# Expert weights loaded as whole matrices into four places instead of quarters into sixteen

## The reference, cut to what matters

```
def expert_choice_moe(h, w_router, w_gate, w_up, w_down):
    ...
    aff = jax.nn.softmax((h @ w_router).astype(jnp.float32), axis=-1)
    gates, idx = lax.top_k(jnp.swapaxes(aff, 1, 2), cap)
    xg = jax.vmap(lambda hb, ib: hb[ib])(h, idx)
    a = jax.nn.silu(jnp.einsum("becd,edf->becf", xg, w_gate)) * jnp.einsum("becd,edf->becf", xg, w_up)
    yo = jnp.einsum("becf,efd->becd", a, w_down) * gates[..., None].astype(h.dtype)
    return jax.vmap(lambda ib, vb: jnp.zeros((s, d), vb.dtype).at[ib.reshape(-1)].add(vb.reshape(-1, d)))(idx, yo)
```

## Time and profile before

| | |
|---|---|
| median of three runs | 2006.61 us |
| the profiled execution's own time | 2004.85 us |
| its span | 2003.0 us |
| PE busy | 1871.0 us, 93% |
| DMA, whole span | 162 GB/s |
| first expert matmul starts | 763.10 us |
| last expert matmul ends | 1214.99 us |
| DMA from 775 to 1200 us | 420 to 422 GB/s in every stretch of 25 us |

### The profile page before, as it was taken

How to read it: one execution, slowest core, us unless ns; L and a number is a source line. 1 busy time by engine, 2 the same in 40 slices (tenths; PEclk the granted TensorE clock), 3 DMA queues, 4 the chain that set the end, 5 groups by cost and what they waited for, 6 DMA issues and landing times.

```text
span 2003.0 us, 20796 instructions
## 1 busy us (share of the span) xinstructions
PE 1871.0 (93%) x8818; PEld 1327.0 (66%) x8818; DVE 849.2 (42%) x1108; ACT 557.3 (28%) x737; POOL 0.2 (0%) x4
## 2 busy tenths in 40 slices
PE   5999999999999969998998887989979999999997
PEld 4788766688897753443444335887867778777785
DVE  5544255534472460110111114566745654344445
ACT  4222334433253321110101013344323332213131
POOL 0000000000000000000000000000000000000000
PEclk8999999999999989999999999989988999999999
DMA  4322211032353176999999994222211222232321
GB/s 143 106 95 92 77 48 35 22 107 85 105 159 107 51 294 264 421 421 422 421 420 421 422 420 162 83 65 84 79 48 43 84 83 86 84 105 84 97 92 42
DMA packets 148212, 324.51 MB, mean 162 GB/s; under 512 B 8721, under 2 KB 118433, under 8 KB 123553
## 3 DMA queue, kind: packets, MB, share of 16 engines
q1 hardware_dynamic: 148128, 323.30, 43.5%
HBM read 321.18 MB, written 2.10 MB: 161 GB/s over the span
## 4 chain that ended last, share of the span: by engine, by line
PE 81%; DMA 9%; DVE 6%; ACT 3%; issue 1%; SPq 0%; DVEq 0%; ACTq 0%
PE bank L531 18%; PE bank L532 18%; PE bank L533 18%; PE bank L939 11%; DMA ew_d<-in_w_exp_up 3%; DMA ew_b<-in_w_exp_up 3%; PE bank L904 2%; PE bank L714 1%; ACT w_hi L1234 1%; DVE w_lo L1664 1%; PE bank L690 1%; DMA raw<-in_w_exp_up 1%; DMA ew_d<-in_w_exp_down 1%; PE bank L962 1%; PE bank L1125 1%
## 5 line engine op out<-in xcount | busy, mean ns | idle before, releaser
L1664 DVE TENSOR_TENSOR w_lo<-raw,w_hi 128x2048 fp32r<-128x2048 f32 x107 | 245.1, 2291 | 257.9 <-ACT w_hi L1234 232.0
L531 PE MATMUL bank<-H_hi,w_hi 128*128 128x512 f32 (+1 forms) x832 | 330.8, 398 | 24.9 <-DVE H_lo L1664 22.0
L532 PE MATMUL bank<-H_lo,w_hi 128*128 128x512 f32 (+1 forms) x832 | 324.5, 390 | 0.0
L533 PE MATMUL bank<-H_hi,w_lo 128*128 128x512 f32 (+1 forms) x832 | 324.2, 390 | 0.0
L531 PEld LDWEIGHTS bank<-H_hi,w_hi 128*128 128x128 f32 x832 | 158.4, 190 | 77.7 <-issue 26.6
L1234 ACT ACTIVATE w_hi<-raw 128x2048 fp32r<-128x2048 f32 x77 | 146.8, 1907 | 132.1 <-PE bank L533 123.5
L533 PEld LDWEIGHTS bank<-H_hi,w_lo 128*128 128x128 f32 x832 | 158.4, 190 | 35.4
L532 PEld LDWEIGHTS bank<-H_lo,w_hi 128*128 128x128 f32 x832 | 158.7, 191 | 34.3 <-issue 1.0
L531 PE MATMUL bank<-C_hi,w_hi 128*128 128x512 f32 x384 | 154.3, 402 | 6.5 <-DVE X L2314 6.5
L533 PE MATMUL bank<-C_hi,w_lo 128*128 128x512 f32 x384 | 152.4, 397 | 0.0
L532 PE MATMUL bank<-C_lo,w_hi 128*128 128x512 f32 x384 | 152.4, 397 | 0.0
(11 more groups left out here) (386 smaller groups left out, 2649.0 us busy)
## 6 DMA issues: line engine op xcount, KB each, us to landing
raw<-in_w_in SPq DMA_DIRECT2D x38, 1024.0 KB, 5.5
raw<-in_w_ff SPq DMA_DIRECT2D x32, 1024.0 KB, 5.4
ew_b<-in_w_exp_gate SPq DMA_DIRECT2D x16, 1024.0 KB, 26.4
ew_b<-in_w_exp_up SPq DMA_DIRECT2D x16, 1024.0 KB, 26.1
ew_c<-in_w_exp_up SPq DMA_DIRECT2D x16, 1024.0 KB, 26.9
ew_b<-in_w_exp_down SPq DMA_DIRECT2D x16, 1024.0 KB, 26.6
ew_c<-in_w_exp_gate SPq DMA_DIRECT2D x16, 1024.0 KB, 27.8
ew_c<-in_w_exp_down SPq DMA_DIRECT2D x16, 1024.0 KB, 27.6
```

The costliest lines, as they stand in the source:

```text
L531: pe.matmul(o, lhs[0], rhs[0], start=first, stop=False)
L532: pe.matmul(o, lhs[0], rhs[1], start=False, stop=False)
L533: return pe.matmul(o, lhs[1], rhs[0], start=False, stop=last)
L1664: return dve.tensor_tensor(out=dst, in0=src, in1=hi_part.bitcast(F32), op=ALU.subtract)
```

## The change

A load is now a whole matrix of 4 MB: partition p gets rows 8p to 8p + 7, 32 KB in a row. `EUNITS` is 6 loads to a pair, `ESLOTS` is 4 places of 4 MB, in the same 16 MB of bytes: place 0 is `raw` and `ew_e` (two halves in different tiles, so always loaded in halves), place 1 the new tile `ew_da` over `ew_d` and `ew_a`, places 2 and 3 `ew_b` and `ew_c`. `cuts(g)` says in which pieces a matrix is loaded: quarters in unit 2 and in the last two units, halves in units 3 to 5 and for matrices in place 0 and matrix 1, and whole for the others. A piece of unit u waits until the steps of unit u - 2 that read the same quarters are done; a whole matrix waits until all four are. PE's steps wait for the piece in which their quarter comes (`LANDED`). Since a partition now holds eight rows that follow each other, the transposes take every eighth column of SG (`D:KT`, from `4 * half + i`), and the first `hidden_turn` of a pair waits for both halves of SG instead of one.

```diff
-EUNITS = 24
-ESLOTS = 16
+EUNITS = 6
+ESLOTS = 4
+def cuts(g):
+    u, last = g // 2, EPAIRS * EUNITS // 2 - 1
+    if u == 2 or u >= last - 1:
+        c = [0, 1, 2, 3, 4]
+    elif u in (3, 4, 5) or g % ESLOTS == 0 or g == 1:
+        c = [0, 2, 4]
+    else:
+        c = [0, 4]
+    return list(zip(c, c[1:]))
+LANDED = {}
+_loads = [0] * (4 * ESLOTS)
+for _g in range(EPAIRS * EUNITS):
+    for _a, _b in cuts(_g):
+        _s = 4 * (_g % ESLOTS) + _a
+        _loads[_s] += 1
+        for _q in range(_a, _b):
+            LANDED[(_g, _q)] = (_s, 16 * _loads[_s])
...
-        ew_a = place("ew_a", [P, 2, 8 * UC], F32, R + 80 * K)
+        ew_da = place("ew_da", [P, 4, 8 * UC], F32, R + 64 * K)
         ew_e = place("ew_e", [P, 2, 8 * UC], F32, R + 108 * K)
         ew_b = place("ew_b", [P, 4, 8 * UC], F32, ew_at)
         ew_c = place("ew_c", [P, 4, 8 * UC], F32, R)
-        ew_d = place("ew_d", [P, 2, 8 * UC], F32, R + 64 * K)
...
-        ew_in = [sem(f"ew_in{i}") for i in range(ESLOTS)]
+        ew_in = [sem(f"ew_in{i}") for i in range(4 * ESLOTS)]
...
-        def expert_slot(g):
+        def expert_slot(g, a, b):
 
             s = g % ESLOTS
-            if s < 2:
-                return ew_a[:, s, :]
-            if s < 4:
-                return raw[:, s - 2, :]
-            if s < 6:
-                return ew_e[:, s - 4, :]
-            if s < 10:
-                return ew_b[:, s - 6, :]
-            return ew_c[:, s - 10, :] if s < 14 else ew_d[:, s - 14, :]
+            if s == 0:
+                return raw[:, a:b, :] if b <= 2 else ew_e[:, a - 2:b - 2, :]
+            return (ew_da, ew_b, ew_c)[s - 1][:, a:b, :]
...
-                        q, j = 2 * half + i // 2, i % 2
-                        ins = pe.transpose(bank[4 + half][:, i * P:(i + 1) * P],
-                                           SG[:, q * 256 + j:(q + 1) * 256:2], ident[:, :])
+                        ins = pe.transpose(bank[4 + half][:, i * P:(i + 1) * P], SG[:, 4 * half + i:D:KT], ident[:, :])
...
             def expert_step(p, w, q, lhs, acc):
 
                 views = []
                 for e in range(2):
-                    g = EUNITS * p + 8 * w + 2 * q + e
-                    pe.wait_ge(ew_in[g % ESLOTS], 16 * (g // ESLOTS + 1))
-                    views.append(expert_slot(g).rearrange("p (j n) -> p j n", j=2))
+                    g = EUNITS * p + 2 * w + e
+                    s, landed = LANDED[(g, q)]
+                    pe.wait_ge(ew_in[s], landed)
+                    views.append(expert_slot(g, q, q + 1).rearrange("p o (j n) -> p (o j) n", j=2))
...
             def hidden_turn(p, half):
 
-                pe.wait_ge(a_ready, 2 * p + half + 1)
+                pe.wait_ge(a_ready, 2 * p + 2)
                 o = up_banks(p)[half]
                 for i in range(4):
-                    q, j = 2 * half + i // 2, i % 2
-                    ins = pe.transpose(o[:, i * P:(i + 1) * P], SG[:, q * 256 + j:(q + 1) * 256:2], ident[:, :])
+                    ins = pe.transpose(o[:, i * P:(i + 1) * P], SG[:, 4 * half + i:D:KT], ident[:, :])
                 mark(ins, ("at", p, half))
...
-            experts = [t[n].rearrange("o e (q p j) f -> (o e) q p (j f)", q=4, p=P, j=2)
+            experts = [t[n].rearrange("o e (p j) f -> (o e) p (j f)", j=KT)
                        for n in ("w_exp_gate", "w_exp_up", "w_exp_down")]
-            for g in range(EPAIRS * EUNITS):
-                p, w, q, e = g // EUNITS, g % EUNITS // 8, g % 8 // 2, g % 2
-                if g >= ESLOTS:
-                    b = g - ESLOTS
-                    done(sp, ("mu", b // EUNITS, b % EUNITS // 8, b % 8 // 2))
-                elif g < 2:
-                    done(sp, ("mla_out", KT - 1))
-                elif g < 4:
-                    sp.wait_ge(w_lo_ready, U0["zk"])
-                elif g < 6:
-                    done(sp, ("mla_out", KT - 1))
-                elif g < 14:
-                    done(sp, ("mem_out", KT - 1))
-                else:
-                    done(sp, ("tk", TT - 1, 1))
-                sp.dma_start(expert_slot(g), experts[w][2 * p + e, q]).then_inc(ew_in[g % ESLOTS], 16)
+            def expert_load(g, a, b):
+                p, w, e = g // EUNITS, g % EUNITS // 2, g % 2
+                dst = expert_slot(g, a, b).rearrange("p q n -> p (q n)")
+                src = experts[w][2 * p + e][:, a * 8 * UC:b * 8 * UC]
+                sp.dma_start(dst, src).then_inc(ew_in[LANDED[(g, a)][0]], 16)
+            done(sp, ("mla_out", KT - 1))
+            expert_load(0, 2, 4)
+            expert_load(1, 2, 4)
+            sp.wait_ge(w_lo_ready, U0["zk"])
+            expert_load(0, 0, 2)
+            done(sp, ("mem_out", KT - 1))
+            expert_load(2, 0, 4)
+            expert_load(3, 0, 4)
+            done(sp, ("tk", TT - 1, 1))
+            expert_load(1, 0, 2)
+            for u in range(2, EPAIRS * EUNITS // 2):
+                b = 2 * u - ESLOTS
+                pieces = cuts(2 * u + 1)
+                for a, z in pieces:
+                    done(sp, ("mu", b // EUNITS, b % EUNITS // 2, z - 1))
+                    for e in range(2):
+                        for c, d in cuts(2 * u + e):
+                            if a <= c and d <= z:
+                                expert_load(2 * u + e, c, d)
```

## The result

The changed kernel takes 2023.9 us (median of four runs, 2021.5 to 2029.3) against 2006.7 for the kernel before on the same chip: 1.0087 times as long, interval 1.0066 to 1.0109. Run again beside other experiments it gave 1.0105 (1.0087 to 1.0122). By these two comparisons the change makes the kernel 17 to 21 us slower. I forecast 2024, in 2012 to 2034.

The account below looks back on a forecast made before the run. Coarse release makes up loads wait for the long down unit; PE's chain, 20.4 + 21.9 + 13.8 + 2.2 + 5.05 = 63.4 us a pair against 60, ends the stage 17.3 us later: 2024 us, range 2012 to 2034.

Parts of the forecast that it names:

- What bounds the stage: Expert stage: the 20.4 us down unit outlasts the next load (19.5), so up loads are asked late and PE idles 8.2 us.
- One sign: Sign of being right: in the plateau, DMA is below 400 GB/s in slices of 50 us.
- The PE chain: From one down unit to the next, through up load, up unit, clock loss and scatter: 63.4 us a pair.
- The DMA chain: From one down unit to the next: 20.4 + 2.4 + 2 x 19.5 = 61.8 us a pair, shorter than PE's.
- the clock's term: Up unit after 8.2 us of idle: first 4.4 us at half clock, costing 2.2 us, bounds 0 and 4.4.
- the clock holds: Rival, up units: no clock fall, so the DMA chain decides at 61.8 us a pair; +8.7, 2015 us; chance 0.13.
- 32 KB in a row: Whole-matrix loads: longer rows cut a unit's 8 MB from 19.9 us to between 19.9 and 19.4, taken as 19.5.
- faster: Rival, expert loads: long rows speed DMA enough to repay lost overlap, deciding from 453 GB/s on; chance 0.05.
- The start: Start of the stage: first loads cost 0; pair 0's first hidden turn waits for SG's second half, 0.7 us more.
- The end: Last expert step: ends at 1232.3 instead of 1215.0, a cost of 17.3 us; nothing moves behind it.
- The transposes: Turns reading every eighth column of SG: cost taken as 0, upper bound 3.2 us a pair; slow-transposes rival chance 0.08.
- The rule on large loads: Skill's rule: 1 MB reaches 78% of peak, 16 MB 97%; forecast said the trace disagrees where loads queue, 422 GB/s.

Follow-up runs that it names:

- e1: The changed kernel with every matrix from unit 2 on loaded in quarters: 2005.2 us, 0.9999 times the kernel before.
- e7: The kernel before, units 6 to 21: loads wait until the unit two back is wholly done, PE until its unit has all landed: 2030.9 us, ratio 1.0126.
- e12: The changed kernel, loads unchanged, with the previous pair's scatter ahead of the up unit and the next pair's route right behind it: 2011.0 us, ratio 1.0026.
- e4: The changed kernel with 32 unused matmuls ahead of the up unit in pairs 2 to 6, keeping PE busy: 2025.4 us, 1.0109 times the kernel before.
- halves: The changed kernel with units 6 to 21 loaded in halves of 2 MB instead of whole matrices: 2000.7 us, 0.9976 times the kernel before.

## Why the prediction was right

**What bounds the stage: right.** The down unit, with route and feature turn in it, lasts 20.4 us, longer than the unit behind it takes to load; only then are the next up matrices asked for. SP's issue stands at the end of each down unit (1123.98, 1123.99). The quarters (e1) show that it is the size, the pair of edges on the kernel before (e7) that size means release and start together, and e12 that the distribution of PE's work decides most of what it costs. One sign was too strict: the slices of 50 us were to be below 400 GB/s, and they are 379 to 413.

**The PE chain: right, term by term.** 20.4 + 21.9 + 13.8 + 2.2 + 5.05 = 63.4 was the forecast; the cycle shown has 20.4 + 22.1 (with SP's issue and 0.14) + 16.2 + 5.0 = 63.8, the mean is 63.6. The up unit's surplus is 1.6 to 2.9 us, 2.4 in the mean, where I took 2.2.

**The DMA chain: too small.** I had 61.8 and put the PE chain above it by 1.6. With the clock held (e4) a pair still takes 63.2. Two terms are off, by that run's own view (397 GB/s at a share of 93.4%). Dead time: 6.6% of 63.2 are 4.2 us a pair, where 61.8 - 3 x 19.5 = 3.3 were worked out. Data: 397 at 93.4% are 425 GB/s while packets run, 19.7 us a unit and not 19.5, so 0.6 a pair. The two chains are within 0.4 us of each other, so the clock's term could be struck out and the time would stand: that the clock decides the last 1.6 us a pair, as I had it, isn't borne out. The rival "the clock holds", 2015 us, was wrong in its time for this reason, and I gave it 0.13. In the changed kernel itself the missing 4.6 us a pair are about what my PE chain leaves, 63.4 - 58.5 = 4.9.

**32 KB in a row: right where nothing disturbs it.** The rate was to go from 421 to 430 (D = 19.5). The changed kernel's four stretches of 56 us between two gaps (872 to 928, 936 to 992, 1000 to 1056, 1063 to 1119) have 425, 429, 432 and 428 GB/s; the third of them:

```profile
1000.00:1056.00 56.00, 47.45 (x220) 21.05 (x217) 7.20 (x14) 3.55 (x6) 0.00 (x0) 0.94 1.01 432
```

Over all the time in which packets run it is 423 (393 at 92.8%), since around the gaps some packets take longer. Neither comes near the 453 that the rival "faster" asked for.

**The start: nearly right.** I took 0.7 us for the first hidden turn; it waited 1.5 us against 0.87 before, so 0.6. Not foreseen was a wait of 1.6 us at the gate unit of pair 2: I counted whole matrices from unit 7 on, but `cuts` already loads the second matrix of unit 6 whole, and it landed at 869.76. The up unit's data, asked for at 868.31, queued behind it. Up of pair 2 started at 891.6, forecast 890.7; up of pair 6 at 1146.1, forecast 1144.3.

**The end: 1234.95, forecast 1232.3**, and 1234.2 in the second profile. The stage became 20.5 and 18.3 us longer, forecast 17.3. The median agreed with mine to 0.1 us partly by luck: the first profile's stage ended 2.7 us later than forecast while its rest took 3.3 us less than before, and the second comparison puts the cost at 1.0105, or 21 us.

**The transposes: right, cost 0.** Groups of weight loads in the changed kernel, for the hidden and the feature turn:

```profile
L961 PEld LDWEIGHTS bank<-ident,SG 128*128 128x128 f32 x64 | 9.4, 190 | 3.6 <-DVE SG L2032 2.3
...
L936 PEld LDWEIGHTS bank<-ident,SG 128*128 128x128 f32 x56 | 6.8, 194 | 5.7 <-issue 5.7
```

Every eighth column loads in 190 to 194 ns, no slower than every second. The rule that I quoted from the Trainium skill (SBUF — State Buffer, in the section on the DMA port swizzle), two hits in a 16-byte line for full speed, does not show in this operation.

**The rule on large loads.** The Trainium skill (DMA: Bandwidth & Descriptors, Measured) ranks 16 MB above 1 MB. Where loads queue, the sizes of this case differ by 3% at most: 421 GB/s for loads of 1 MB (8 KB in a row), 428 for halves, 425 to 432 for whole matrices between two gaps.

## What to carry to other kernels

With two places for a unit of data, most of what a coarse load costs comes from a coarse release together with a coarse start (in e12, with that mended, 5 us were left of 21), and it comes where a unit's stay (from its landing to its last reader) is longer than the time in which the next unit loads, or within a few microseconds of it. Work out that stay for every unit, with all that the reader does in between, before choosing a size, and again for all of them after moving work; here halves kept the longer rows and lost the coupling. When two chains are within a few per cent of each other, taking one away shows nothing: name the second before pricing the first.

## What the runs showed that I had not expected

- A queue that runs empty costs more than its latency. With the clock held (e4) 4.2 us of DMA time were missing a pair where 3.3 were worked out. And to keep it from running empty, the next load has to be asked for some 2.4 us before the first of the 16 engines is through (e12); the landing, which comes with the last one, was up to 4.4 us later than that.
- A longer row gains little more. The usual packet takes 0.313 us for 8 KB, 0.611 for 16 KB and 1.213 for 32 KB, on 16 engines 419, 429 and 432 GB/s. But with whole matrices some packets take longer where units meet, and the mean over the time in which packets run is 423 (in e12 419 at a share of 99.1%).
- The clock can fall after the wait is over. In e12 the first matmul takes 1.09 us after a wait of 3.90 us (928.85). After one of 4.29 us the first takes 0.62 (1169.74), but those from 1170.62 on take 0.96 and 1.06, until 1174. A look at the first matmul alone would have missed that.
